# Attention heads in pairs on the two row halves of TensorE, with the probabilities transposed two steps behind their scores

## The reference

```python
h = x @ w_in                                   # (n, 1024) @ (1024, 3328)
qa, ka, va, ga, qb, kb, vb, gb = split(h)
qa, ka = rope(qa), rope(ka)                    # A heads: one rotation
out_a = dilated_attention(qa, ka, va) * silu(ga)
qb, kb = axial_rope(rms_norm(qb)), axial_rope(rms_norm(kb))
out_b = softmax(qb @ kb.T / 8) @ vb * silu(gb) # 8 query heads, 2 key/value heads
f = concat(out_a, out_b) @ w_out               # (n, 1024) @ (1024, 1024)
y = layer_norm(alpha * x + f, ln_g, ln_b)
```

## Time and profile before

| what | value |
|---|---|
| time before, median of 3 runs | 475.74 us (475.21 to 476.89) |
| span of the profiled execution | 474.6 us; its own time is not given apart, the median of the runs lies 1.1 us above the span |
| TensorE (PE) busy | 438.0 us, 92% of the span |
| DVE, POOL, ACT busy | 301.4, 248.1 and 230.7 us |
| TensorE busy from 135 to 347 us | 211.11 of 212 us |

### The profile page before, as it was taken

One profiled execution on the slowest core, in us unless ns is written; L12 is line 12 of the kernel. 1 busy time (PEld: TensorE's weight loads), 2 busy tenths in 40 slices (PEclk: granted clock), 3 DMA queues, 4 the chain that ended last, 5 costly groups with the idle time before them and its releaser, 6 DMA issues.

```text
span 474.6 us, 8965 instructions
## 1 busy us (share of the span) xinstructions
PE 438.0 (92%) x3292; PEld 413.2 (87%) x3292; DVE 301.4 (64%) x826; ACT 230.7 (49%) x519; POOL 248.1 (52%) x340
## 2 busy tenths in 40 slices
PE   1999979998899999999999999999999789999990
PEld 1999969987799999998899999999888678999990
DVE  1543675339987788664577877855586777433664
ACT  3332113335456565666565565655675876121222
POOL 1126953795554746334346565653543773454664
PEclk9999989999899999999999999999999989999997
DMA  6611212110200101102010010110200136231222
GB/s 237 255 45 52 71 35 74 39 46 23 68 23 23 46 23 36 56 24 66 14 54 23 24 46 24 40 51 23 68 1 23 44 111 245 88 95 42 78 100 89
DMA packets 23291, 30.00 MB, mean 63 GB/s; under 512 B 1872, under 2 KB 19408, under 8 KB 23248
## 3 DMA queue, kind: packets, MB, share of 16 engines
q1 hardware_dynamic: 22816, 29.30, 19.0%
q10 hardware_dynamic: 432, 0.13, 0.1%
HBM read 26.28 MB, written 3.15 MB: 62 GB/s over the span
## 4 chain that ended last, share of the span: by engine, by line
PE 66%; POOL 10%; DVE 10%; issue 7%; ACT 3%; DMA 2%; SPq 1%; ACTq 0%; DVEq 0%; POOLq 0%
PE bank L504 15%; PE bank L505 15%; PE bank L506 15%; PE bank L465 9%; PE bank L593 6%; POOL scr L1062 3%; DVE prob L870 2%; PE bank L551 2%; PE bank L552 2%; DMA h<-x_prompt 2%; DVE tmp_s L796 1%; POOL tanh L1048 1%; ACT prob L707 1%; DVE p_lo L878 1%; POOL w_lo L1032 1%
## 5 line engine op out<-in xcount | busy, mean ns | idle before, releaser
L504 PE MATMUL bank<-w_hi,t_lo 128*128 128x256 f32 x576 | 168.2, 292 | 1.9 <-DVE nmax L870 0.8
L506 PE MATMUL bank<-w_hi,t_hi 128*128 128x256 f32 x576 | 164.0, 285 | 0.0
L505 PE MATMUL bank<-w_lo,t_hi 128*128 128x256 f32 x576 | 163.9, 285 | 0.0
L504 PEld LDWEIGHTS bank<-w_hi,t_lo 128*128 128x128 f32 x576 | 111.5, 194 | 3.1 <-DVE nmax L870 1.0
L505 PEld LDWEIGHTS bank<-w_lo,t_hi 128*128 128x128 f32 x576 | 111.6, 194 | 0.1
L506 PEld LDWEIGHTS bank<-w_hi,t_hi 128*128 128x128 f32 x576 | 111.3, 193 | 0.0
L1032 POOL TENSOR_TENSOR w_lo<-raw,w_hi 128x512 fp32r<-128x512 f32 x52 | 67.2, 1302 | 59.2 <-ACT w_hi L659 59.1
L1113 POOL TENSOR_SCALAR prob<-prob,den 128x512 f32<-128x512 f32 (+1 forms) x96 | 60.5, 635 | 68.6 <-DVE den L899 68.5
L707 ACT ACTIVATE prob<-prob,nmax 128x512 f32<-128x512 f32 (+1 forms) x96 | 62.3, 649 | 54.1 <-DVE nmax L870 53.6
L878 DVE TENSOR_TENSOR p_lo<-bank,p_hi 128x512 fp32r<-128x512 f32 x80 | 54.8, 685 | 3.0 <-ACT p_hi L716 2.2
L659 ACT ACTIVATE w_hi<-raw 128x512 fp32r<-128x512 f32 x62 | 37.6, 622 | 34.6 <-DMA raw<-w_in 17.4
(11 more groups left out here) (97 smaller groups left out, 784.3 us busy)
## 6 DMA issues: line engine op xcount, KB each, us to landing
raw<-w_in SPq DMA_DIRECT2D x50, 256.0 KB, 2.8
raw<-w_out SPq DMA_DIRECT2D x16, 256.0 KB, 2.9
h<-x_prompt SPq DMA_DIRECT2D x7, 512.0 KB, 6.8
h<-x_sample SPq DMA_DIRECT2D x4, 512.0 KB, 9.6
y_prompt<-h SPq DMA_DIRECT2D x8, 256.0 KB, 2.1
y_sample<-h SPq DMA_DIRECT2D x4, 256.0 KB, 2.1
cst<-consts SPq DMA_DIRECT2D x1, 960.0 KB, 9.5
h<-x_prompt SPq DMA_DIRECT2D x2, 256.0 KB, 3.8
```

The source lines that it names most:

```text
L504: nc.tensor.matmul(out, a_lo, b_hi, start=(m == 0), stop=False)
L505: nc.tensor.matmul(out, a_hi, b_lo, start=False, stop=False)
L506: ins = nc.tensor.matmul(out, a_hi, b_hi, start=False, stop=(m == KT - 1))
```

## The change

Two heads now form a pair, and the loop runs over 40 steps of two units. The high and low parts of the queries stand in tensors of their own (`q_hi`, `q_lo`), head s of a pair on partitions 64 s to 64 s + 63, and the keys likewise. Scores of a pair are six matmuls of 64 rows: three passes, each for both heads in turn, head 0 on the upper row half into one bank, head 1 on the lower into the other. Both score banks are therefore written in every step, and scores(w) wait for both masks of step w - 1. Staging is done for a pair at a time with blocks 128 wide; `double_keys` is gone, and for pair 0 the shared B keys are written four times (`twice`: two key heads, each to both halves). Transposes of a step stand two steps behind its scores (`LAG = 2`), `prob` is a ring of six, and `values` stand in the same step as the last transposes that they need, with one output bank for each head; the second of these banks is also the staging bank `t_ps`, so `values` of head 1 wait for the staging of their step and staging waits for `mix`. `mix` multiplies by the gate once for a pair. Buffers are laid over each other to make room; the tables `BESIDE`, `SPLIT_AT` and `WIDE_AT` are written anew.

```diff
+PAIRS = HEADS // 2
+PAIRS_B = N_HEADS_B // 2
+NW = PAIRS * UNITS
 
 GROUPS = QT // 2 + 1
-PRING = 4
+PRING = 6
 CONSTS_AFTER = 2
 DVE_LOW_CHUNKS = (0, 1, 2, 3)
-LAG = 3
-STEPS = NU + LAG + 1
-
-
-
-BESIDE = ((0, 5), (3, 8), (55, 44), (62, 50), (65, 52), (72, 54))
-
-SPLIT_STEPS = (73, 75, 77, 79, 80, 81, 82)
-
-WIDE_AT = {76: ((0, (0, 1)),), 78: ((1, (0, 1)),), 80: ((2, (0, 1)), (0, (2, 3))), 81: ((1, (2, 3)),),
-           82: ((3, (0, 1)), (2, (2, 3))), 83: ((3, (2, 3)),)}
+LAG = 2
+STEPS = NW + LAG + 1
+
+
+
+BESIDE = ((0, 5), (2, 9), (26, 44), (30, 50), (33, 52), (36, 54))
+
+SPLIT_AT = {37: (4, 5), 38: (6, 7), 39: (0, 1), 41: (2,)}
+
+WIDE_AT = {38: ((0, (0, 1)), (1, (0, 1))), 39: ((2, (0, 1)), (3, (0, 1))),
+           40: ((0, (2, 3)), (1, (2, 3)), (2, (2, 3)), (3, (2, 3))),
+           41: ((4, (0, 1, 2, 3)), (5, (0, 1, 2, 3)))}
...
-            def t_batch(b):
+            def t_batch(b, w=0):
                 n = t_count[b]
                 if n:
+                if sums_before(w):
+                    pe.wait_ge(mixed, sums_before(w))
...
-            def scores(u):
-                j, k = divmod(u, UNITS)
-                kv = head_columns(j)[4]
+            def scores(w):
+
+                p, k = divmod(w, UNITS)
                 if k == 0:
-                    pe.wait_ge(t_lo_done, staged[j])
-                if u >= 2:
-                    pe.wait_ge(s_masked, u - 1)
-                out = s_ps[u % 2]
-                q = q_st[:, j % 2, :]
-                if k < QT:
-                    nc.tensor.matmul(out[:], q[:, k * P:(k + 1) * P], k_lo[:, kv % 2, 0:SEQ], start=True, stop=False)
-                    ins = nc.tensor.matmul(out[:], q[:, k * P:(k + 1) * P], k_hi[:, kv % 2, 0:SEQ],
-                                           start=False, stop=True)
-                else:
-                    for t in range(ST):
-                        o = out[:, t * DEC_SEQ:(t + 1) * DEC_SEQ]
-                        lhs = q[:, SEQ + t * P:SEQ + (t + 1) * P]
-                        nc.tensor.matmul(o, lhs, k_lo[:, kv % 2, SEQ:TOK], start=True, stop=False)
-                        ins = nc.tensor.matmul(o, lhs, k_hi[:, kv % 2, SEQ:TOK], start=False, stop=True)
-                ins.then_inc(s_ready, 1)
-
-            def prob_transposes(u):
-                pe.wait_ge(scaled, u + 1)
-                if u >= 2:
-                    pe.wait_ge(pt_lo_done, u - 1)
-                transpose_batch(pt_ps[u % 2], [prob[:, u % PRING, n * P:(n + 1) * P] for n in range(4)]) \
+                    pe.wait_ge(t_lo_done, staged[p])
+                if w:
+                    pe.wait_ge(s_masked, 2 * w)
+                blocks = [(k * P, 0, SEQ, 0)] if k < QT else \
+                    [(SEQ + t * P, SEQ, TOK, t * DEC_SEQ) for t in range(ST)]
+                for n, (q0, k0, k1, at) in enumerate(blocks):
+                    for r, (q, key) in enumerate(((q_lo, k_hi), (q_hi, k_lo), (q_hi, k_hi))):
+                        for s in range(2):
+                            rows = slice(HEAD_DIM * s, HEAD_DIM * (s + 1))
+                            ins = nc.tensor.matmul(s_ps[s][:, at:at + k1 - k0], q[rows, p % 2, q0:q0 + P],
+                                                   key[rows, key_slot(p), k0:k1], start=(r == 0), stop=(r == 2))
+                            if r == 2 and n == len(blocks) - 1:
+                                ins.then_inc(s_ready, 1)
+
+            def values(G, s, step):
...
+                w = UNITS * p + min(2 * k + 1, QT)
                 sample = k == GROUPS - 1
-                pe.wait_ge(pt_lo_done, u + (1 if sample else 2))
+                pe.wait_ge(pt_lo_done, 2 * w + s + 1)
+                if s:
+                    pe.wait_ge(t_lo_done, batches_through(step))
...
-                for m, tiles in WIDE_AT.get(u, ()):
+            for w in range(STEPS):
+                if w < NW:
+                    scores(w)
+                if LAG <= w < NW + LAG:
+                    for s in range(2):
+                        prob_transposes(2 * (w - LAG) + s)
+                for b in steps[w]:
+                    t_batch(b, w)
+                for m, tiles in WIDE_AT.get(w, ()):
                     wide_tile(m, tiles)
-                for b in steps[u]:
-                    t_batch(b)
-                if LAG <= u < NU + LAG:
-                    prob_transposes(u - LAG)
-                for item in items_at(u):
+                for item in items_at(w):
                     project(*item)
-                for g in groups_at(u):
-                    values(g)
-            for m in range(KT // 2, KT):
+                for G in groups_at(w):
+                    for s in range(2):
+                        values(G, s, w)
+            for m in range(6, KT):
...
+
+            def twice(a, z, c0, c1):
+                return [(a, z, slice(HEAD_DIM * kv, HEAD_DIM * (kv + 1)),
+                         of((k_hi, k_lo), kv, c0, c1, slice(HEAD_DIM * s, HEAD_DIM * (s + 1))))
+                        for kv in range(N_KV_B) for s in range(2)]
...
+            for w in range(STEPS):
+                if w < NW:
+                    for s in range(2):
+                        mask_max(2 * w + s)
+                for s in range(2):
+                    if LAG <= w < NW + LAG:
+                        prob_low(2 * (w - LAG) + s)
+                    if w < NW:
+                        invert(2 * w + s)
+                for b in steps[w]:
...
```

More of the change, by code:

```diff
@@ L271, in build, with staging @@
         beside = [item for item in items if ALONE <= item[0] < IN_CHUNKS]
[L275 to L278 removed]
+        def staging(p):
+            return [("q", p)] + ([("k", p)] if p == 0 or p >= PAIRS_B else []) + [("r", p)]
         def items_before(u):
@@ L382, in y_rows @@
             return y_prompt[t * P:(t + 1) * P, :] if t < QT else y_sample[(t - QT) * P:(t - QT + 1) * P, :]
[L384 to L387, removed]
+        steps = {w: [] for w in range(STEPS)}
+        for p in range(PAIRS - 1):
+            for n, b in enumerate(staging(p + 1)):
+                steps[UNITS * p + (0, 2, 3)[n]].append(b)
         first = staging(0)
@@ L404, in groups_at, with unit @@
[L404 to L410, removed]
-        def transposed_at(u):
-            return group_of(u) % 2, u % UNITS % 2
+        split_steps = {w: [split_order.index(k) for k in tiles] for w, tiles in SPLIT_AT.items()}
+        def unit(v):
+            w, s = divmod(v, 2)
+            return *divmod(w, UNITS), s
@@ new lines, in group_of, with groups_at, batches_through, sums_before @@
+        def group_of(v):
+            p, k, s = unit(v)
+            return 2 * (GROUPS * p + k // 2) + s
+        def groups_at(w):
+            p, k = divmod(w - LAG, UNITS)
+            return [GROUPS * p + k // 2] if 0 <= w - LAG < NW and (k % 2 or k == QT) else []
+        def batches_through(w):
+            return len(first) + sum(len(steps[n]) for n in range(w + 1))
+        def sums_before(w):
+            return sum(len(groups_at(n)) for n in range(w))
+        def rows_of(v):
+            k = unit(v)[1]
+            return [(k, 0, SEQ)] if k < QT else [(QT + t, t * DEC_SEQ, (t + 1) * DEC_SEQ) for t in range(ST)]
@@ new lines, in t_batch @@
+                what, p = b
+                (qs, qc), (ks, kc) = queries(p), keys(p)
+                if what == "q":
+                    pe.wait_ge(rope_added, chunk_end(ropes, heads_chunk(2 * p, "q")))
+                    pieces = [qs[:, t, qc:qc + P] for t in range(QT)]
+                elif what == "k":
+                    pe.wait_ge(rope_added, chunk_end(ropes, heads_chunk(2 * p, "k")))
+                    pieces = [ks[:, t, kc:kc + P] for t in range(QT)]
+                else:
+                    pieces = [qs[:, QT + t, qc:qc + P] for t in range(ST)]
+                    if p == 0 or p >= PAIRS_B:
+                        pieces += [ks[:, QT + t, kc:kc + P] for t in range(ST)]
@@ new lines, in prob_high, with copy_low @@
+            def prob_high(v):
+                act.wait_ge(pt_ready, v + 1)
+                p, k, s = unit(v)
+                if k % 2 == 0 and v >= 2:
+                    act.wait_ge(pv_done, group_of(v - 2) + 1)
+                nc.scalar.activation(p_hi[:, s, k % 2, :], pt_ps[s][:], ACT.Copy).then_inc(pt_hi_done, 1)
+            def copy_low(G):
+                for s in range(2):
+                    act.wait_ge(pv_done, 2 * G + s + 1)
+                    nc.scalar.activation(o_lo[HEAD_DIM * s:HEAD_DIM * (s + 1), :],
+                                         o_ps[s][HEAD_DIM:P, 0:2 * P], ACT.Copy).then_inc(low_copied, 1)
@@ new lines, in mix @@
+            def mix(G):
+                p, k = divmod(G, GROUPS)
+                for s in range(2):
+                    o = o_lo[HEAD_DIM * s:HEAD_DIM * (s + 1), :]
+                    dve.wait_ge(low_copied, 2 * G + s + 1)
+                    ins = nc.vector.tensor_tensor(o, o_ps[s][0:HEAD_DIM, 0:2 * P], o, ALU.add)
+                after(ins)
```

(2 more changed lines are left out.)

389 lines of the change are left out of this document (177 added, 212 removed).

## The result

The changed kernel takes **485.06 us** (median of 4 runs, 483.14 to 486.33); the kernel before, on the same chip, 476.31 (4 runs, 475.21 to 477.66). The ratio is 1.0177, 95% interval 1.0147 to 1.0207: slower, where 467.3 us and faster were forecast. The profiled execution is the slowest of the four (486.33 us); it spans 484.5 us, 9.9 more than the earlier trace rows.

The account below looks back on a forecast made before the run. TensorE was taken as the bound from 135 to 347 us, with DVE counting at front and end. 474.6 - 7.2 - 3.2 + 0 + 3.5 + 1.5 + 0 - 3 = 466.2 us span, so 467.3 us; range 461 to 484.

Parts of the forecast that it names:

- Changing the tile: Each step's switch from 128-row to 64-row tiles and back on TensorE: taken as 0, at most 9.9 us.
- second rival: TensorE empties itself at each change of tile: +9.9 us, 477 us, no measurable change or slower; chance 0.17.
- Scores: Score matmuls on two row halves side by side, weight loads not: 0.58 us less a pair, -3.2 us.
- first rival: Row halves of the score matmuls don't run side by side: 486 us, slower; chance 0.18.
- fourth rival: Weight loads of the two row halves overlap as well: 464 us; chance 0.08.
- Staging: TensorE transposes for queries and keys fall from 156 to 78, 66 of them in the middle stretch: -7.2 us.
- First staging: Pair 0's B keys copied four times ahead of the loop: waits of 2.4 and 1.1 us, +3.5 us.
- New waits in the middle: Values wait on DVE's p_lo in the step of their last transposes: +1.5 us, bounds 0 and 11.
- Front: Start of the loop, where DVE's norm work decides: taken as 0, bounds -3 and +3 us.
- End: Loop's end and last tiles: DVE multiplications and TensorE scores saved, 1.8 us bare: -3 us, bounds -4.5 and 0.
- step from span to time: Median of the runs taken to lie 1.1 us above the profiled span, from 466.2 to 467.3 us.

Follow-up runs that it names:

- Experiments 2: Changed kernel with one of each step's eight 128-row transposes moved between the first and second score pass, four tile changes a step instead of two: 496.78 us, ratio 1.0421.
- experiment 9: Changed kernel with each step's scores as three matmuls on all 128 rows, both heads summed, so no change of tile: 474.20 us, ratio 0.9950.
- experiment 5: Changed kernel with two of the three score passes of every second head left out: 484.49 us, ratio 1.0157.
- experiment 1: Changed kernel with pair 0's key batch two projection items earlier, ahead of the query batch: 480.33 us, ratio 1.0094.
- Experiment 7: As experiment 6, with the last ten input items spread so every step with values from 26 to 36 has one ahead: 471.86 us, ratio 0.9900.
- experiment 6: Changed kernel with the early keys of experiment 1 and one more projection item ahead of the loop and by step 2: 477.50 us, ratio 1.0025.

## Why the prediction was wrong, step by step

**The step that failed is "Changing the tile"**: "At least it costs nothing ... That is the nearest row, and I take 0". The row on which it rested, values alternating between 128x128 and 128x64 tiles at no cost, holds after the change too, but there the columns change. A change of rows costs 0.30 to 0.34 us a step for the way in and out, in 27.5 steps 8.3 to 9.4 us, near the upper bound of 9.9. Experiments 2 and 9 show it from both sides. The second rival had the mechanism and the price, and its sign, a gap of 0.1 us at the first L597 and at the next transpose, is there (0.09 and 0.10). I let a row on another dimension overrule it. The Trainium skill, TensorEngine Tiling (Array Packing), section Tiling Modes, had the rule, that a change of tiling mode drains TensorE. The trace agrees in that no load and no matmul goes ahead across the change; that the array is empty then it can't show, since the ends of matmuls are modelled (the one of 205.72 is shown up to 206.00, the next begins at 205.93).

**Scores.** The first rival, halves not side by side, is refuted (experiment 5). That its 486 us lies so near the 485 measured is chance. The loads of the halves overlap too, the fourth rival: a sample step's passes follow each other 0.12 us apart, so the term is -6.4 for the -3.2 taken, a miss in my favour. With the changes of tile a pair's scores cost 4 x 0.99 + 1.00 = 4.96 us, 0.32 more than before's 4.64, not 0.58 less.

**Staging.** -7.2 over six pairs fits. No run has it by itself, but experiment 9 has it without the changes of tile: its pairs 1 to 5 take 180.77 us, 11.7 less than before with equal items. Its scores, 4 x 0.70 + 0.72 a pair, make 5.6 of that; 6.1 are left, 1.2 a pair.

**First staging.** The mechanism was right, the size a little low. The wait of 2.4 is 2.95 us. That of 1.1 is hidden in the changed kernel's profiled execution because the item over it runs at half pace; in experiment 9, where it doesn't, it is 1.14. Together 4.1, against +3.5; the stretch shows +5.4 here and +4.0 where the clock stays at 1.00, and experiment 1 got 4.7 back.

**New waits in the middle.** The middle up to 335 us shows none. All lie in pair 6, where the table leaves steps 30 and 33 without an item: 0.63, 1.20, 0.63 and 1.32, 3.8 us where 1.5 were taken, within the bounds of 0 to 11. The reason given ("cover and chain are nearly equal where a step has one item") holds; the sum did not take in steps with none. Experiment 7 puts items there, and these waits are gone.

**Front.** Taken as 0, it is +2.7. The values' wait came a step earlier, as feared in the same sentence, and fell on the norm work, as experiment 6 shows; but its longest grew only from 2.3 to 3.5 us. The larger part goes with the changes of tile in pair 0's own steps, which the rival did not count: experiment 9 takes 45.71 us for the pair, 2.0 less, with the same wait of 3.5.

**End.** -3 forecast, +1.6 found. The 1.8 us bare ahead of the last tile came as worked out (L970, 1.8). But DVE's saved multiplications bought nothing, for TensorE waits there on chains of several engines (t_lo of POOL 2.4, of DVE 1.8, p_lo 1.8, masks 1.4): 8.0 us of waits from step 35 on, 6.3 before. The changes of tile have 0.9 of it (113.80 in experiment 9).

Together: pairs 1 to 5 missed their forecast by 4.8 us; their 25 steps paid 7.6 for changes of tile (188.34 against 180.77 in experiment 9) and got 2.9 from the loads. The smaller terms, nearly all on the losing side and in part changes of tile too, turned the second rival's 477 into 485. The step from span to time, 1.1, was small as well: each run here lies 1.8 above its own span (486.33 and 484.5). Experiment 7 takes away the waits of the first staging, of the front and of pair 6, not those of the end, and stands 4.7 us below the kernel before, with the changes of tile still in it.

## What to carry to other kernels

Pack matmuls on half the rows only in blocks long enough to pay for one way in and out: here that was 0.30 to 0.34 us a step, and packing saved 0.23 (two units before stream 0.92, a step after 0.69). Count changes of row tile as a cost of their own, and changes of column tile (128x128 to 128x64 here) as none. When a change halves the loop's steps, the table that hands out covering work has to be made anew: each step with values and no item ahead of them waited here (steps 30, 33 and 36). And a price taken from the nearest row must change the same thing as the edit does.

## What the hardware showed that I had not expected

- The change between 128-row and 64-row tiles: the next matmul 0.09 to 0.10 us late on each way, and the first load behind it bare (0.10 us for the 64-row pass, 0.05 for the transposes). It can't be told from these runs whether a change between two kinds of row tile other than these costs the same.
- The two row halves start their matmuls independently, and not in the order of the program: in experiment 5 a matmul written fourth started 0.01 us after the first. The count that the mask waits for still came only behind the third (mask at 216.20, third matmul at 215.77). The Trainium skill, TensorE: Matmul & The Clock Gate, section Part 3, has matmuls start strictly in program order; the trace differs in the starts.
- Weight loads on the two halves run side by side: the two loads of a pass fill one row of 0.19 us, as long as a single load, and in a sample step a pass of two loads and two matmuls takes 0.12 us.
